# A mixture-of-experts stage fed by one DMA queue: the down pieces moved to ScalarE's own queue

## The reference, cut to what matters

```python
def swiglu(h, wg, wu, wd):
    return (jax.nn.silu(h @ wg) * (h @ wu)) @ wd

def moe_swiglu(h, w_router, wg, wu, wd):
    t = h.reshape(B * S, D)
    logits = (t @ w_router).astype(jnp.float32)
    top_vals, top_idx = lax.top_k(logits, TOP_K)
    w = jax.nn.softmax(top_vals, axis=-1)
    gates = jnp.sum(jax.nn.one_hot(top_idx, N_EXPERTS) * w[..., None], axis=1)
    # sum over experts e of gates[:, e] * swiglu(t, wg[e], wu[e], wd[e])
```

## Time and profile before

| | us |
|---|---|
| median of 3 runs | 1497.09 |
| lowest, highest | 1495.69, 1499.86 |
| the profiled execution's own time | 1501.24 |
| its span in the profile | 1499.4 |

### The profile page before, as it was taken

One profiled execution on the slowest core, in us unless ns is written; L12 is line 12 of the kernel. 1 busy time (PEld: TensorE's weight loads), 2 busy tenths in 40 slices (PEclk: granted clock), 3 DMA queues, 4 the chain that ended last, 5 costly groups with the idle time before them and its releaser, 6 DMA issues.

```text
span 1499.4 us, 26492 instructions
## 1 busy us (share of the span) xinstructions
PE 1464.3 (98%) x12004; PEld 935.2 (62%) x12004; DVE 517.3 (35%) x716; ACT 393.0 (26%) x461; POOL 36.7 (2%) x49
## 2 busy tenths in 40 slices
PE   9999999999999999999999999999999989999987
PEld 7888888888888888743654445643447533356325
DVE  7885755545466876530111101101100111010014
ACT  6576553443455665410000000000000000000004
POOL 0100000000000100020000000000000000000000
PEclk9999999999999999999999999999999999999999
DMA  9544455555455344789999999999999999999991
GB/s 340 190 140 161 165 196 197 196 180 187 167 201 181 136 168 169 305 320 424 408 409 428 425 427 422 411 428 427 425 427 424 425 428 426 426 425 404 428 396 60
DMA packets 78711, 468.57 MB, mean 313 GB/s; under 512 B 6588, under 2 KB 10316, under 8 KB 54028
## 3 DMA queue, kind: packets, MB, share of 16 engines
q1 hardware_dynamic: 77804, 465.92, 78.2%
q0 software_dynamic: 624, 0.74, 0.2%
q10 hardware_dynamic: 176, 0.27, 0.1%
HBM read 465.70 MB, written 1.07 MB: 311 GB/s over the span
## 4 chain that ended last, share of the span: by engine, by line
PE 88%; DMA 7%; DVE 4%; issue 1%; ACT 1%; SPq 0%; DVEq 0%; ACTq 0%
PE ps L1765 49%; PE ps L1753 11%; PE ps L1755 11%; PE ps L1754 11%; DMA ring<-in_w_moe_down 6%; PE ps L1762 1%; PE ps L1760 1%; PE ps L1761 1%; PE ps L1768 1%; DMA raw<-in_w_in 1%; DVE x L1612 1%; PE ps L2088 0%; DVE w_lo L1102 0%; DVE arena L1625 0%; PE ps L1929 0%
## 5 line engine op out<-in xcount | busy, mean ns | idle before, releaser
L1765 PE MATMUL ps<-ring,arena 128*32 128x448 f32 (+3 forms) x6260 | 640.1, 486 | 15.1 <-DMA ring<-in_w_moe_down 12.8
L1765 PEld LDWEIGHTS ps<-ring,arena 128*32 128x32 f32 (+1 forms) x6260 | 289.6, 116 | 360.9 <-issue 297.8
L1102 DVE TENSOR_TENSOR w_lo<-raw,w_hi 128x2048 fp32r<-128x2048 f32 x99 | 226.1, 2290 | 125.2 <-ACT w_hi L747 125.1
L1753 PE MATMUL ps<-w_hi,hT_hi 128*128 128x512 f32 (+1 forms) x640 | 250.5, 391 | 3.4 <-DVE hT_lo L1184 1.4
L1755 PE MATMUL ps<-w_hi,hT_lo 128*128 128x512 f32 (+1 forms) x640 | 246.7, 385 | 0.0
L1754 PE MATMUL ps<-w_lo,hT_hi 128*128 128x512 f32 (+1 forms) x640 | 246.4, 385 | 0.0
L747 ACT ACTIVATE w_hi<-raw 128x2048 fp32r<-128x2048 f32 x99 | 189.3, 1914 | 110.8 <-PE ps L1755 105.3
L1625 DVE TENSOR_TENSOR arena<-arena,ps 128x896 f32<-128x896 f32 x20 | 21.8, 1088 | 419.6 <-PE ps L1765 419.6
L1765 PE MATMUL ps<-arena 128*32 128x32 f32 (+11 forms) x2220 | 146.1, 352 | 7.2 <-DVE arena L1581 2.9
L1753 PEld LDWEIGHTS ps<-w_hi,hT_hi 128*128 128x128 f32 x640 | 120.6, 188 | 28.6 <-issue 3.1
L1755 PEld LDWEIGHTS ps<-w_hi,hT_lo 128*128 128x128 f32 x640 | 120.6, 188 | 24.3
(11 more groups left out here) (308 smaller groups left out, 881.4 us busy)
## 6 DMA issues: line engine op xcount, KB each, us to landing
ring<-in_w_moe_gate SPq DMA_DIRECT2D x56, 1792.0 KB, 16.5
ring<-in_w_moe_up SPq DMA_DIRECT2D x56, 1792.0 KB, 18.8
ring<-in_w_moe_down SPq DMA_DIRECT2D x24, 2048.0 KB, 23.9
ring<-in_w_moe_down SPq DMA_DIRECT2D x31, 1536.0 KB, 23.1
raw<-in_w_in SPq DMA_DIRECT2D x37, 1024.0 KB, 7.0
raw<-in_w_dense_gate SPq DMA_DIRECT2D x14, 1024.0 KB, 5.1
raw<-in_w_dense_up SPq DMA_DIRECT2D x14, 1024.0 KB, 5.1
raw<-in_w_dense_down SPq DMA_DIRECT2D x14, 1024.0 KB, 4.9
```

Of the source, the lines that this page charges most:

```text
L1102: nc.vector.tensor_tensor(w_lo[:, n % SLOTS, :], raw[:, raw_at(n), :], w_hi[:, n % SLOTS, :].bitcast(F32), ALU.subtract).then_inc(low_read ...
L1753: nc.tensor.matmul(o, x_parts[0][x_cols], parts[0], start=first, stop=False)
L1765: return nc.tensor.matmul(o, lhsT, rhs, start=start, stop=stop, skip_group_check=second_in_bank)
```

## The change

SyncE's program keeps the gate and up pieces (and the two pieces ahead for the second item). Every other down piece is issued by ScalarE, in a new function `load_downs`, which stands behind the Silu of the item, with the same condition as before: down u when up u is used. The loop over pairs on ScalarE is written out (a Python loop in place of `Fori`), since the second item leaves out two pieces. ScalarE now waits for `routed` ahead of the first item's down pieces.

```diff
-    def expert_pieces(gate, up, down):
+    def down_pieces(down):
...
+        return [piece for q in range(QUARTERS) for piece in downs_of(q)]
...
-            for n in range(UP0 + 1, DOWN0 + 1):
-                if n == DOWN0:
-                    sp.wait_ge(spot_filled[UP0 % SPOTS], 32)
-                else:
-                    sp.wait_ge(pieces_used, BEHIND[n] + 1)
+            for n in range(UP0 + 1, DOWN0):
+                sp.wait_ge(pieces_used, BEHIND[n] + 1)
                 load_expert(n, first[n])
...
-            for n in range(DOWN0 + 1, ITEM_PIECES):
-                sp.wait_ge(pieces_used, BEHIND[n] + 1)
-                load_expert(n, first[n])
-            for n, source in enumerate(second):
-                if n not in SECOND_AHEAD:
-                    sp.wait_ge(pieces_used, ITEM_PIECES + BEHIND[n] + 1 if n in BEHIND else BEHIND_BEFORE[n] + 1)
-                    load_expert(n, source)
+            for n, source in enumerate(second[:DOWN0]):
+                sp.wait_ge(pieces_used, ITEM_PIECES + BEHIND[n] + 1 if n in BEHIND else BEHIND_BEFORE[n] + 1)
+                load_expert(n, source)
             with sp.Fori(1, later_items) as t:
...
-                for n, source in enumerate(chosen_pieces(e)):
+                for n, source in enumerate(chosen_pieces(e)[:DOWN0]):
...
+                def load_downs(i, at, ahead=()):
+                    e = act_e.value_load(item_expert_i[0:1, bass.ds(i, 1)], min_val=0, max_val=EXPERTS - 1)
+                    chosen_down = w_moe_down[0, bass.ds(e, 1), :, :].rearrange("e k n -> (e k) n")
+                    for u, source in enumerate(down_pieces(chosen_down)):
+                        if DOWN0 + u not in ahead:
+                            act_e.wait_ge(pieces_used, at(ITEM_PIECES, UP0 + u + 1))
+                            act_e.dma_start(down_piece(u), source).then_inc(spot_filled[(DOWN0 + u) % SPOTS], 16)
...
-                with act_e.Fori(0, PAIRS - 1) as t:
+                for t in range(PAIRS - 1):
                     big, small = of_pair(t, BIG), of_pair(t, SMALL)
                     item(BIG, big)
+                    if t == 0:
+                        act_e.wait_ge(routed, 1)
+                    load_downs(2 * t, big)
                     take_y(BIG, big)
                     take_next(big, SMALL)
                     item(SMALL, small)
+                    load_downs(2 * t + 1, small, SECOND_AHEAD if t == 0 else ())
                     take_y(SMALL, small)
                     take_next(small, BIG)
-                act_e.wait_ge(routed, 1)
                 tail = act_e.value_load(n_items_i[0:1, 1:2], min_val=1, max_val=EXTRA + 1)
                 with act_e.Fori(0, tail) as t:
                     extra = of_extra(t)
                     item(BIG, extra)
+                    load_downs(t + TAIL, extra)
...
                 final = of_extra(tail)
                 item(SMALL, final)
+                load_downs(tail + TAIL, final)
```

More of the change, by code:

```diff
@@ L152, in build_trunk, with downs_of @@
     assert HALF <= BANK and ROWS_EACH == 7 and KD == 2 * QUARTERS == 8
+    def down_pieces(down):
+        def downs_of(q):
+            neighbours = down[q * QUARTER:(q + 1) * QUARTER, :].rearrange("(p r) n -> p r n", r=ROWS_EACH)
+            return [neighbours[:, js[0]:js[-1] + 1, :] for js in DOWN_ROWS]
+        return [piece for q in range(QUARTERS) for piece in downs_of(q)]
     def expert_pieces(gate, up, down):
@@ L157, in rows_of @@
             return [w[k * P:(k + 1) * P, :] for k in range(KD)]
[L159 to L163, removed]
+        return rows_of(gate) + rows_of(up) + down_pieces(down)
     DOWN_SIZE = [len(DOWN_ROWS[u % 2]) * D for u in range(2 * QUARTERS)]
```

## The result

| us | before | with the change |
|---|---|---|
| median | 1497.03 (4 runs) | 1517.12 (4 runs) |
| lowest, highest | 1495.69, 1499.86 | 1514.53, 1518.91 |
| the profiled execution's own time | 1501.24 | 1515.52 |
| its span | 1499.4 | 1513.7 |

The ratio of the times is 1.0129, with a 95% interval of 1.0117 to 1.0141: slower by 20 us. The forecast was 1514, in a range of 1499 to 1537.

The account below looks back on a forecast made before the run. The expert stage was taken as DMA-bound. Delays of +5.5, +8.5 and +5.8 us start item 8 19.8 late, leaving +15.1; with +1.9 for clock, +17 gives 1518.2 profiled, 4.15 above the median: 1514 us, range 1499 to 1537.

Parts of the forecast that it names:

- Half and half: While both ScalarE's and SyncE's queues have work, each gets half of the DMA engines, so the last up pieces arrive at half speed.
- two parts or one part of three: Bounds for ScalarE's queue's share: two of three leaves about the same pair time; one of three gives about +45, 1542 us.
- rival 1: Whole kernel: nothing changes, 1497 us, as engines nearly keep issue order or early down pieces repay the up pieces' loss; chance 0.12.
- Rival 2: Whole kernel faster, expected 1490 us, floor 1477: two queues fill gaps that one leaves, raising the rate above 426 GB/s; chance 0.08.
- The pair: One big and one small item in the steady state: 214.6 us in place of 208.9, with small-item waits of 3.6 and 10.8.
- The dry spell: At each big item's end the DMA engines run out of queued pieces, some 6 us dry, time lost for good.
- Item 2: Early small item with its first two down pieces elsewhere: up 7 lands at 814.1, wanted at 808.6, so +5.5 us.
- The sum: Delays through the expert stage: item 8 starts 19.8 us late, +15.1 remains at its end, +17 in all, 1518.2 profiled.
- the clock: TensorE's granted clock falls where it waits; about four more such stretches add +1.9 us together, bounds 0 and 6.
- the step from profile to median: The profiled execution stands 4.15 us above the median of the runs, so 1518.2 becomes a predicted 1514 us.
- The big item: A big item starts with 22 us of gate pieces landed and TensorE slower than the transfers, so it waits for nothing.
- The signs: Expected: 215 us pairs, 3 to 6 us waits at up 7, changed landing delays, DMA share below 0.9, equal queue shares.

## Why the prediction was right

**What bounds the kernel, and the share.** The reading that a small item is bound by transfers and that the order of their service decides held. Half and half was 53.8 to 46.9 in item 4 and 51.2 to 49.5 in item 6. The bounds of two parts or one part of three for the second queue aren't needed, and rival 1 falls: the early down pieces do not repay what the up pieces lose. Rival 2 falls too: two queues together moved 424 to 429 GB/s, never more than one. The rule of the Trainium skill that issuing elsewhere only saves issuing time (DMA: Bandwidth & Descriptors, "Issuing engines are not separate DMA queues") gives 1497 by itself; the measurement is 20 us from it, and the same section's remark that such transfers interleave is the half that counts here.

**The pair.** Forecast 214.6 for the pairs 4 to 6 and 6 to 8, measured 215.2 and 214.9. The parts inside are less exact. Up 7 was to be 3.6 us late and down 7 10.8; in item 6 TensorE waits 6.2 for up and 4.6 for down pieces. Up 7 landed 51.7 us after the item's start (1204.98 + 27.42 - 1180.67) and not 48.9: up 4, the last piece ahead of the sharing, was 2 us behind my count by its landing record. The halving would make 4 of these 2 on an engine that is as late as the last one; the first was 1.8 us ahead of it, and 2.8 came of it. What TensorE loses at up 7 it no longer has to wait for at down 7, which landed at 85.3, near the 86.9 forecast. The two waits are 10.8 together rather than 14.4; the slow clock behind them fills up the rest: 16 matmuls for 4.61 in place of 3.23, 12 for 4.46 in place of 2.80, 3.0 us in item 6. Over items 4, 6 and 8 the groups at the lower clock cost 8.8 us, where four such groups (7.93 in place of 6.47) cost 5.8 before: 3.0 more, and the prediction had 1.9. So the pair came out by two errors that cancel, waits 3.6 us too long and a clock that was left out of the pair's own sum; that they are of one size is luck.

**The dry spell.** "Some 6 us" at the end of each big item was 6.2 by the bytes in item 5, and most of it stands where it was to stand, at 1143 to 1153 us.

**Item 2** was the pair that was mis-sized most, +5.5 forecast and +3.1 measured. When down 2 began to flow, the stream was further ahead than in the trace before (by its landing record up 5, the last piece ahead of the sharing, came 1.4 us earlier, counted from the item's start), so less of up 7 was left to be halved; TensorE waited 2.0 us for it, and for 0.6 at down 7.

**The sum.** Up to the split of the last weights it was 15.1, with the clock 17.0; measured 14.4 between the two profiles. Item 8 was to start 19.8 us late and started 17.2 late, and like the forecast it gave some of that back. The profiled executions alone would have given 1515.5 where 1518.2 was forecast. The median came out 3 us above the forecast, since the step from profile to median took over the 4.15 us of one execution; the next profile was 1.6 us below its median instead. The stage was 2.7 us shorter than forecast and this step 5.8 larger; that the two went opposite ways is luck, and a forecast from one profile carries some 5 us of this kind.

**The big item** was said to wait for nothing, and in the change it doesn't. It holds because its gate pieces are ahead, though less than I counted: I had the last one landed 14 us after the item's start, and it was 16.7. The experiments show that this is no property of the big item: with its down pieces alone on the second queue it waits 6 us. My forecast of 1496 to 1502 for that kernel failed for that step.

**The signs** that were named came, with one exception: up 7 landed 27 to 31 us after issue in items 4, 6 and 8, and big item 5's down pieces under 20 after theirs (13 to 15 by their landing records). Of the page's slices only the one at the end of item 5 is under 0.9; in slices of 7.5 us (the DMA view of 1100 to 1400 us) the lowest at the ends of items 5 and 7 are at 0.5 and 0.4. The exception is the wait at up 7 of 3 to 6 us in every small item: it is 3.1, 5.2 and 5.1 in items 4, 6 and 8, but 2.0 in item 2.

What stays open is the remainder of the cost with everything held in order, 7 us in the median. The windows above show one hold that loses about 2 us of transfer (four windows at half the rate), and there are two in an item; a kernel with order and without such gaps would need a signal for "nearly landed", and none was tried.

## What to carry to other kernels

When transfers are the bound and memory lets you issue well ahead, a queue is also a schedule: what stands first is served first. A second queue divides the rate between what is wanted now and what is wanted later. I would expect it to pay only where the first queue has gaps; here it had none, and no kernel tested that. So look at the busy share of the DMA engines before splitting a stream, and count how much of the urgent data is still out when the second queue begins. Repairing it by waits for landings costs gaps of its own; a single queue gives the order without them.

## What the hardware showed that I had not expected

The 16 engines drift apart. By the landing records of each piece, in the kernel before the first engine is done with a piece 5.3 to 6.9 us ahead of the last one in small item 6, longer than a whole piece takes (4.3); with the change it is 2.2 us in the median there, though 4.2 in big item 5. One queue that never runs empty seems to let the fast engines run ahead, and a dry spell to level them; no kernel tested that by itself. What the windows at the hold do show is its price: a wait for a landing empties many engines before it lets the next transfer go.

The effects of the two kinds of item, +19.5 and +10.7 us alone, make +20 together. In a stage that is bound by one stream, the pair's length is its data plus its dry time, and a second disturbance in the same pair mostly moves the first. This is how I read it; the kernels show the sums, not the single steps.
